# Modulation vectors of a two-block float32 kernel: in column groups, and most of them inside the first input projection

## The reference

```python
m_l = jnp.split((jax.nn.silu(c) @ mod_w[i] + mod_b[i])[:, None, :], 6, -1)      # block 1
hl = _modulate(x, m_l[0], m_l[1])          # layer norm, * (1 + scale) + shift
yl = _hyena(hl, ...)                       # input projection 1024 -> 3072, short and long convolutions, output projection
x  = _ln_affine(ALPHA * x + (1.0 + m_l[2]) * yl, ...)
hl = _modulate(x, m_l[3], m_l[4])
x  = _ln_affine(ALPHA * x + (1.0 + m_l[5]) * _expert_choice_moe(hl, ...), ...)

m_lat = jnp.split(sc @ ada_w[l] + ada_b[l], 6, axis=-1)                         # block 2, condition c
m_ctx = jnp.split(scc @ ada_w[l] + ada_b[l], 6, axis=-1)                        # block 2, condition c_ctx
h_lat = modulate(rms_norm(x, norm1_g[l]), m_lat[0], m_lat[1])                   # then mixer, experts, final norm
```

## Time and profile before

| | |
|---|---|
| median of three runs | 4993.97 us (4990.66 to 4994.40) |
| the profiled execution | 4985.86 us |
| its span, first to last instruction | 4984.2 us |
| TensorE busy (PE) | 4086.8 us, 82% |
| VectorE busy (DVE) | 1827.0 us, 37% |
| ScalarE busy (ACT) | 734.3 us, 15% |
| mean granted TensorE clock | 0.914 of full |
| bytes read from HBM | 692.5 MB |
| setup stage | 0 to 159.6 us |
| first projection | 159.6 to 546.7 us |

### The profile page before, as it was taken

One profiled execution on the slowest core, in us unless ns is written; L12 is line 12 of the kernel. 1 busy time (PEld: TensorE's weight loads), 2 busy tenths in 40 slices (PEclk: granted clock), 3 DMA queues, 4 the chain that ended last, 5 costly groups with the idle time before them and its releaser, 6 DMA issues. The chain is left out here.

```text
span 4984.2 us, 55127 instructions
## 1 busy us (share of the span) xinstructions
PE 4086.8 (82%) x22522; PEld 2294.5 (46%) x22522; DVE 1827.0 (37%) x2640; ACT 734.3 (15%) x1507; POOL 977.9 (20%) x789
## 2 busy tenths in 40 slices
PE   6999765666488899999999997499966899584995
PEld 2444554555343244444444443255444888342442
DVE  3132488888833500000000001444065666234003
ACT  0100111111011000000000000212124333111110
POOL 0000376556620000000000000100021555300110
PEclk9999887888789999999999998799977999796997
DMA  6212100010043788887888885221111000305994
GB/s 228 104 69 94 66 36 36 36 72 36 17 190 117 266 303 320 298 314 289 314 305 301 303 301 209 81 71 60 54 56 64 4 4 4 133 34 196 332 322 164
DMA packets 298090, 773.12 MB, mean 155 GB/s; under 512 B 9400, under 2 KB 40112, under 8 KB 290734
## 3 DMA queue, kind: packets, MB, share of 16 engines
q1 hardware_dynamic: 272434, 656.65, 35.5%
q0 software_dynamic: 24352, 103.06, 6.2%
q10 hardware_dynamic: 1116, 10.71, 0.5%
HBM read 692.50 MB, written 77.88 MB: 155 GB/s over the span
## 5 line engine op out<-in xcount | busy, mean ns | idle before, releaser
L1266 PE MATMUL banks<-moe_ring,moe_xeT 128*128 128x512 f32 x2560 | 1122.2, 594 | 4.4 <-ACT moe_xeT L1320 4.4
L1266 PEld LDWEIGHTS banks<-moe_ring,moe_xeT 128*128 128x128 f32 x2560 | 484.4, 191 | 596.6 <-issue 596.6
L1286 PE MATMUL banks<-moe_ring,moe_hidT 128*128 128x512 f32 x1280 | 565.7, 595 | 21.6 <-ACT moe_hidT L1327 21.6
L1356 DVE TENSOR_TENSOR moe_hid<-moe_silu,banks 128x512 f32<-128x512 f32 x80 | 55.0, 687 | 1294.5 <-PE banks L1266 1294.5
L1286 PEld LDWEIGHTS banks<-moe_ring,moe_hidT 128*128 128x128 f32 x1280 | 240.6, 190 | 320.1 <-issue 290.8
L1235 POOL DMA_INDIRECT d_acc<-moe_ye,chosen x32 | 50.8, 1586 | 1688.9 <-DVE moe_ye L1360 1688.9
L1552 PE MATMUL banks<-hT,w_in_ring 128*128 128x512 f32 (+3 forms) x976 | 362.8, 535 | 4.3 <-ACT hT L1575 4.3
L322 PE MATMUL banks<-hT,w_in_ring 128*128 128x512 f32 x768 | 335.5, 596 | 4.3 <-ACT hT L334 4.3
L521 PE MATMUL banks<-y_folded,dft 128*128 128x256 f32 x512 | 128.1, 417 | 231.0 <-DVE y_folded L687 231.0
L1552 PEld LDWEIGHTS banks<-hT,w_in_ring 128*128 128x128 f32 (+1 forms) x976 | 183.0, 188 | 183.8 <-issue 171.5
L962 PE MATMUL banks<-w_out,mix 128*128 128x512 f32 x512 | 230.3, 608 | 11.1 <-DMA w_out<-d_w_out 10.3
(11 more groups left out here) (437 smaller groups left out, 5209.3 us busy)
## 6 DMA issues: line engine op xcount, KB each, us to landing
moe_ring<-d_wg SPq DMA_DIRECT2D x80, 2048.0 KB, 12.6
moe_ring<-d_wu SPq DMA_DIRECT2D x80, 2048.0 KB, 17.3
moe_ring<-d_wd SPq DMA_DIRECT2D x80, 2048.0 KB, 7.9
mod_w_ring<-d_mod_w SPq DMA_DIRECT2D x24, 1024.0 KB, 5.5
w_out<-d_ada_w POOLq DMA_DIRECT2D x12, 2048.0 KB, 9.3
w_in_ring<-d_hy_w_in SPq DMA_DIRECT2D x6, 2048.0 KB, 8.6
d_seq<-u_staged POOLq DMA_DIRECT2D x12, 1024.0 KB, 4.1
w_in_ring<-d_w_in SPq DMA_DIRECT2D x5, 2048.0 KB, 10.4
```

The costliest lines, as they stand in the source:

```text
L1266: last = nc.tensor.matmul(m.ps[:, 2 * kind + c, :], xeT[:, k, :], up(c, kind)[:, k, :], start=(k == 0), stop=(k == KT - 1))
L1286: last = nc.tensor.matmul(m.ps[:, Y_BANK + h, :], hidT[:, c, i * P:(i + 1) * P], down(c)[:, i, h * BANK:(h + 1) * BANK], start=(fc == 0 an ...
L1356: nc.vector.tensor_tensor(hid[:, j % 2, :], sg[:, j % 2, :], m.ps[:, 2 + j % 2, :], ALU.mult).then_inc(s.hid, 1)
```

## The change

Both matvecs are done in six groups of 2048 columns: groups 0 to 2 are block 1's vector, 3 to 5 block 2's two. The weights are silu(c) (or the two vectors of block 2 in turn) repeated to 32 columns. The four matmuls of one k write to PSUM partitions 0, 32, 64 and 96 of one bank, each with 512 of the 2048 columns as its moving operand. One copy brings the 128 x 512 rows to SBUF and four small matmuls with picked identity columns turn them into columns in bank 7.

Group 0 stays in the setup stage, as 8 MB in four loads without a wait. Groups 1 to 5 are 20 slots of two k (2 MB each), one behind each of the units 1 to 20 of the projection; their ring of two lies in the memory of x, free after the transposes. The loops over kinds of SyncE, ScalarE and TensorE are written out; turns use two banks instead of four; the turn of a kind's last unit stands behind the next kind's first unit; `dft` is loaded early. The additions for parts 2 to 5 and for block 2 stand at the end of the projection stage. The ada chunks leave `mixer_out_stage`.

```diff
+def matvec(nc, m, lhs, k, w):
+    for j in range(4):
+        last = nc.tensor.matmul(m.ps[32 * j:32 * j + 32, ROW_BANK, :], lhs[:, k, :], w[:, j * BANK:(j + 1) * BANK],
+                                start=(k == 0), stop=(k == KT - 1))
+    return last
+
+def rows_to_columns(nc, m, rows, group):
+    pick = m.ident[:].rearrange("p (j x) -> p j x", j=4)
+    for b in range(4):
+        if group < MOD_GROUPS:
+            out, rhs = mod_columns(m, group)[:, b], pick[:, :, 0]
+        else:
+            out, rhs = ada_columns(m, group - MOD_GROUPS)[:, b], pick[:, :, 0:2]
+        last = nc.tensor.matmul(out, rows[:, b * P:(b + 1) * P], rhs, start=True, stop=True)
+    return last
...
@@ setup_stage, SyncE, ScalarE, TensorE
-            for i in rounds(sp, N_MOD_CHUNKS // RING):
-                at = [settled(sp, i * (RING * MOD_CHUNK) + c * MOD_CHUNK) for c in range(RING)]
-                for slot in range(RING):
-                    sp.wait_ge(used[slot], i)
-                    sp.dma_start(ring[:, slot], m.dram["mod_w"][:, :, ds(at[slot], MOD_CHUNK)]).then_inc(ready[slot], 16)
+            for slot in range(MV_SLOTS):
+                sp.dma_start(ring[:, slot], m.dram["mod_w"][:, slot * MV_SLOT_K:(slot + 1) * MV_SLOT_K, 0:MV_COLS]
+                             ).then_inc(ready[slot], 16)
...
+            act.wait_ge(s.row_mm, 1)
+            nc.scalar.copy(row[:], m.ps[:, ROW_BANK, :]).then_inc(s.row, 1)
+            act.wait_ge(s.var, 1)
+            nc.scalar.activation(rstd[:], rstd[:], ACT.Sqrt).then_inc(s.std, 1)
...
+            for k in range(KT):
+                if k % MV_SLOT_K == 0:
+                    pe.wait_ge(ready[k // MV_SLOT_K], 16)
+                last = matvec(nc, m, m.lhs_mod, k, ring[:, k // MV_SLOT_K, k % MV_SLOT_K, :])
+            last.then_inc(s.row_mm, 1)
+            pe.wait_ge(s.row, 1)
+            rows_to_columns(nc, m, row, 0).then_inc(s.col_mm, 1)
...
@@ hyena_in_stage, SyncE
+            load_w(0, 0)
+            load_w(0, 1)
+            sp.wait_ge(s.hT_mm, 2 * KT)
+            load_mv(0)
+            load_mv(1)
             sp.dma_start(m.dft[:], m.dram["dft"]).then_inc(s.tables, 16)
+            for unit in range(UNITS):
+                kind, mt = unit // MT, unit % MT
+                if mt % 4 == 3 and kind + 1 < KINDS:
+                    sp.wait_ge(s.u_mm, 2 * unit + 2)
+                    load_w(kind + 1, mt // 4)
+                n = slot_of(unit)
+                if n is not None and n + 2 < N_SLOTS:
+                    sp.wait_ge(s.mv_mm, n + 1)
+                    load_mv(n + 2)
...
@@ hyena_in_stage, TensorE
+            def matvec_slot(n):
+                group, kp = 1 + n // MV_SLOTS, n % MV_SLOTS
+                pe.wait_ge(mv_in[n % 2], (n // 2 + 1) * 16)
+                if kp == 0 and group > 1:
+                    pe.wait_ge(s.mv_row, group - 1)
+                lhs = m.lhs_mod if group < MOD_GROUPS else m.lhs_ada
+                for j in range(MV_SLOT_K):
+                    last = matvec(nc, m, lhs, kp * MV_SLOT_K + j, mv_ring[:, n % 2, j, :])
+                last.then_inc(s.mv_mm, 1)
...
+            for unit in range(UNITS):
...
+                if unit:
+                    turn(unit - 1)
+                n = slot_of(unit)
+                if n is not None:
+                    matvec_slot(n)
+                before = slot_of(unit - 1)
+                if before is not None and before % MV_SLOTS == MV_SLOTS - 1:
+                    matvec_columns(1 + before // MV_SLOTS)
+            turn(UNITS - 1)
...
@@ hyena_in_stage, ScalarE and VectorE
+                if n is not None and n % MV_SLOTS == MV_SLOTS - 1:
+                    group = 1 + n // MV_SLOTS
+                    act.wait_ge(s.mv_mm, n + 1)
+                    if group > 1:
+                        act.wait_ge(s.mv_col, group - 1)
+                    nc.scalar.copy(mv_rows[:], m.ps[:, ROW_BANK, :]).then_inc(s.mv_row, 1)
...
+                v.wait_ge(s.u_ready, kind * (2 * MT))
...
@@ mixer_out_stage, TensorE
-            if deep:
-                ada(0)
-                ada(1)
             pe.wait_ge(s.out_read, 2 * TT)
...
-            if deep:
-                for c in range(2):
-                    ada_columns(c)
-                    ada(c + 2)
             pe.wait_ge(s.aff, 1)
```

More of the change, by code:

```diff
@@ L30 @@
 N_MOD = 6 * KT
-MOD_CHUNK = 256
-N_MOD_CHUNKS = 6 * D // MOD_CHUNK
 EMB = 33
@@ L296, in _, with turn @@
             pe.wait_ge(s.hT_ready, 2 * KT)
-            def turn(kind, mt):
-                pe.wait_ge(s.conv, kind * MT + mt + 1)
+            def turn(unit):
+                mt = unit % MT
+                pe.wait_ge(s.conv, unit + 1)
                 for par in range(2):
-                    if 2 * mt + par >= 4:
-                        pe.wait_ge(s.staged, kind * (2 * MT) + 2 * mt + par - 3)
+                    n = 2 * unit + par
+                    if n >= 2:
+                        pe.wait_ge(s.staged, n - 1)
@@ L303, in turn @@
                     for j in range(4):
                         last = nc.tensor.transpose(
-                            m.ps[:, 4 + (2 * mt + par) % 4, j * P:(j + 1) * P],
+                            m.ps[:, 4 + par, j * P:(j + 1) * P],
                             uc[:, mt % 2, 4 * P * (j % 2) + 2 * par + j // 2:4 * P * (j % 2 + 1):4], m.ident[:])
                     last.then_inc(s.tr_mm, 1)
[L309 to L321, removed]
-                            last = nc.tensor.matmul(m.ps[:, g % 4, :], ring[:, c, k, (mt % 4) * P:(mt % 4 + 1) * P],
-                                                    hT[:, k, h * BANK:(h + 1) * BANK], start=(k == 0), stop=(k == KT - 1))
-                        last.then_inc(s.u_mm, 1)
-                    if mt:
-                        turn(kind, mt - 1)
-                turn(kind, MT - 1)
@@ new lines, in matvec_columns @@
+            def matvec_columns(group):
+                pe.wait_ge(s.mv_row, group)
+                rows_to_columns(nc, m, mv_rows, group).then_inc(s.mv_col, 1)
+            for unit in range(UNITS):
+                kind, mt = unit // MT, unit % MT
+                c = mt // 4
+                if mt % 4 == 0:
+                    pe.wait_ge(ready[c], (kind + 1) * 16)
+                for h in range(HALF):
+                    g = 2 * unit + h
+                    if g >= 4:
+                        pe.wait_ge(s.u_ready, g - 3)
+                    for k in range(KT):
+                        last = nc.tensor.matmul(m.ps[:, g % 4, :], ring[:, c, k, (mt % 4) * P:(mt % 4 + 1) * P],
+                                                hT[:, k, h * BANK:(h + 1) * BANK], start=(k == 0), stop=(k == KT - 1))
+                    last.then_inc(s.u_mm, 1)
+                if unit:
[6 more added lines that the diff above has]
+                    matvec_columns(1 + before // MV_SLOTS)
@@ L1019, in _ @@
             last.then_inc(s.at_mm, 1)
-            if deep:
-                for c in range(2, ADA_CHUNKS):
-                    ada_columns(c)
-                    if c + 2 < ADA_CHUNKS:
-                        ada(c + 2)
             pe.wait_ge(s.top, 1)
```

175 lines of the change are left out of this document (76 added, 99 removed).

## The result

| | before | after |
|---|---|---|
| median, same chip | 4992.32 us (4988.88 to 4994.40) | 4927.62 us (4927.05 to 4928.70) |
| ratio, 95% interval | | 0.9871 [0.9854, 0.9888] |
| profiled execution / its span | 4985.86 / 4984.2 | 4927.98 / 4926.3 |

The changed kernel is 1.3% faster: 64.7 us by the medians, 57.9 us between the two profiled executions. Forecast was 4938, in a range of 4924 to 4985.

What follows compares the result with a forecast made beforehand. TensorE was taken to bound setup's end and the projection. Gains of 104.9 us less 7.8 of losses and 41.2 for slots gave 55.9 net off the 4994.0 median: 4938.1 us, 8-in-10 range 4924 to 4985.

Steps and rivals of the forecast that it cites:

- setup shorter: Setup stage: last additions follow VectorE's normalising operation at 88.14, not TensorE's matvec at 158.65; 70.5 us less.
- 20 slots: Projection: column groups run together, 1.72 us a slot plus 0.34 for two drains, 2.06 each, 41.2 us lost.
- experts' cold start: After the router stage: without ada matmuls before them the experts start with TensorE cold, 0.7 us lost.
- The row of two tiles: Trace row: 12 records on two 64 x 64 tiles sharing no rows or columns take 2.79 us; basis for the slot price.
- B: Projection rival, half together: next group starts only beside a matmul's second record; slot 4.2 us, total 4981 us; chance 0.10.
- C: Projection rival: groups on shared rows run one behind the other; slot 7.2 us, total 5045, up to 5062; chance 0.16.
- D: Projection rival: hidden slots wait for their loads, 5 us each, about 5038 us; chance 0.04 together with mixtures.
- A step to columns: Projection: four small matmuls turning rows into columns, five times at 0.95 us each, 4.8 us lost.
- The nine additions: Projection's end: nine small VectorE operations stand behind the last stored wait, 1.3 us lost.
- The cold start: Start of the projection: TensorE stands still before the hT phase's 64 transposes, 1.0 us lost.
- the two borders: Projection, between kinds: two TensorE idle times of 3.67 us go, plus 1.1 for the slower clock; 8.4 us gained.
- The cover at the borders: Projection: next kind's bias is ready some 4 us before its turn; a store 4 us later would use that up.

Runs made afterwards that it cites:

- the kernels of one, two and four groups: Changed kernel with each k's four matmuls sent to one 32-column group (5031.77 us), alternating between two (4959.97 us), or unaltered with four (4927.62 us).
- the kernel with three groups in setup: Changed kernel with block 2's slots moved to the router stage and all three block 1 groups computed in setup: 4897.17 us.
- The eight other kernels: Follow-up variants of the changed kernel, altering group count, issue order, or where block 1's and block 2's vectors are computed; 4891.49 to 5031.77 us.
- the other order of issue: Changed kernel with the group as outer loop in a slot, so two matmuls follow each other on one group: 4927.83 us.
- block 2 back in the router stage, in chunks or in groups: Changed kernel with block 2's vectors computed in the router stage, as the old 12 chunks (4928.91 us) or as 12 column-group slots (4902.04 us).
- two or three groups in setup: Changed kernel with block 2's column-group slots in the router stage and two (4891.49 us) or three (4897.17 us) block 1 groups in setup.
- the groups without the move: Changed kernel with block 1's three groups in setup, block 2's 12 old chunks in the router stage, no projection slots: 4923.47 us.

## Why the prediction was right, step by step

| term | forecast | measured |
|---|---|---|
| setup shorter | 70.5 | 159.56 - 88.64 = 70.9 |
| 20 slots | 41.2 (2.06 each) | 39.6 (1.98 each) |
| projection longer | 40.6 | 423.2 - 387.2 = 36.0 |
| router stretch shorter | 26.7 | 121.39 - 94.75 = 26.6 |
| experts' cold start | 0.7 lost | 12.58 to the first matmul, 12.91 before: 0.3 gained |
| stages with unchanged code | 0 | 7.4 lost, then 3.4 gained |
| profiled executions | 55.9 | 57.9 |

*The slot.* The step on which all hung, that records of different column groups start together although they share all rows, is shown by the kernels of one, two and four groups. The row of two tiles gave the right price, but it could not show this step, since its tiles share no rows: choosing it was a bet, put at 0.70, and it was won. The two drains were too much: 0.13 (1.85 - 1.72) is all that shows from a slot to the next unit, and 1.98 the whole price to ScalarE's evacuations. Rivals B and C fell by the same rows: spacings of 12.1 and 15.1 were theirs, 9.93 was measured. D fell because no idle time is shown at a slot.

The Trainium skill, TensorE: Matmul & The Clock Gate, The mechanism, lets a weight load overlap only when its row group differs. The slot rows do not agree: four groups on the same rows take about a quarter of the time of one, 1.92 us against 7.05 for the same 16 records. The same section names a load into a background weight buffer as a second way; no run here shows whether that is what happens. The Trainium skill, same page, Measured speedup vs the span model, has 2.38 times for three column tiles; here four groups gave 3.8 times and two 1.96, so the measurement decides against carrying that loss over.

*The rest of the projection.* Here the forecast was 4.6 us too dear, and the rows divide it. The slots came 1.6 cheaper. A step to columns costs 0.89: the two evacuations around the first one start at 195.99 and 206.81, 10.82 apart, against 9.93 across a slot alone; five are 4.5 against 4.8. The nine additions were put at 1.3 and cost nothing that shows: from the last store's issue to the stage's end are 5.68 us with them, 5.64 before and in the kernel with three groups in setup, which has none there. TensorE's wait in the last turn rose from 3.69 to 4.38, the 0.7 of the forecast. The cold start held too: the first unit starts 12.64 us into the stage (101.28), 11.57 before, 1.1 against 1.0. The first two units then took 27.73 us and not the 29.43 of before, at a granted clock of 1.00 against 0.94. The eight other kernels have 29.25 to 30.73, among them the one with the other order of issue, whose code is the same up to there, with 29.43. So these 1.7 us are luck of this execution. What remains for the two borders is 8.1 us against 8.4.

*The cover at the borders* held, with about 2 us and not 4, and the rows settle why. From the store's issue to the bias that it releases are 6.9 us at both borders of the changed kernel, where a slot load is issued 0.42 us behind the store (249.91). They are 4.7 at the first border of the kernel before, and 4.8 in the five kernels in which no slot load runs beside it (block 2 back in the router stage, in chunks or in groups; two or three groups in setup; the groups without the move). With the slot load issued 2.1 us behind the store (two groups) they are 5.1, and with 5.5 us (one group) 4.8 again. So a slot load issued right behind the store costs it 2 us, which is the delay the forecast named, at half the size that would have used up the cover. The 5.6 us that the forecast took for the store's landing is the way to the stage's end, about 1.2 longer than the wait for the store (4.4 there); the additions fit into that 1.2.

*Setup and router* came out within 0.4 us of their terms. For the router stage the second block's call of the same function was a measurement of "after" in the trace of before. The 0.7 for the experts' cold start was no price of a cold start: from the first load to the first matmul in block 1 the ten profiles have 12.03 to 12.91, with the 12 chunks ahead of it or without.

*What separates 4938 from 4927.6* is mostly no mechanism. I took the sum off the median of three and so added 8.1 us to what the profiled execution would give. The changed kernel's profiled execution lies 0.4 from its own median, and the one before 6.5 below its median. Of the 10.5 us between forecast and result 8.1 are this step, 2.0 the sum itself (57.9 - 55.9), 0.4 the rest. That the sum is so close is in part luck: its terms were some 6 us too pessimistic (4.6 in the projection, 1.0 at the experts, 0.4 in setup), and the stages with unchanged code lost 4.0 that it did not have.

*The unchanged stages.* The 7.4 us lost between projection and router stage are not the change's doing. Nearly the same code in all ten, from the end of the projection to the start of block 1's last normalising operation, took 1021.0 before, 1028.4 after, and 1020.8 to 1025.6 in the profiles of the eight other kernels. A visible part is the start of the output stage, in the timeline of after and then of the kernel with the other order of issue, whose stage is the same:

```profile
1392.56 8.83 PE L1034 MATMUL banks<-w_out,mix 128*128 128x512 f32 x16 [3.18 <-DMA out_bias<-d_b_out]
```

```profile
1389.79 7.13 PE L1038 MATMUL banks<-w_out,mix 128*128 128x512 f32 x16 [0.91 <-DMA out_bias<-d_b_out]
```

TensorE waits 2.3 us longer for one small transfer in one execution, and the next 16 records take 1.7 longer, at a granted clock of 0.81 in the 9 us from 1392.5, against 1.00 in the same stretch of the other. From the experts' first load to the end the ten profiles have 3291.3 to 3295.1. So the two profiled executions can't be compared below some 7 us outside the stages that the change touches; why TensorE waits longer for this small load in some executions stays open.

## What to carry to other kernels

A matvec should be cut into column groups even when all groups share their rows: the gain is nearly the number of groups, 3.8 for four (measured for float32, 32 columns of weights and 512 moving columns only). Cheap work put on the engine that sets a stage's end is still paid in full: moving block 2's vectors swapped 28 us for 25, while the same slots beside VectorE's selection cost nothing, and the best version (two groups in setup, one in the projection, block 2 under the selection) takes 4891.49 us, 36 below the change and 100 below the kernel before. Before a sum is made against a median, look how far the profiled execution lies from it, and keep that distance as a width of the range and not as a term.

## What the runs showed of the hardware

- A slot on a TensorE that otherwise waits can cost nearly twice: 3.64 us and not 1.92 for the same 16 records. In the kernel with block 2 in groups eight of the twelve slots took 3.35 to 3.64 and four 1.92, two of these behind idle times of 1.62 and 1.91. Its windows around two of the slots have a granted clock of 0.50 (its level of 1.2 GHz) for the one that follows 5.23 us of idle time and scattered work, and 1.00 for one behind dense work. It was hidden there.

```profile
core 0: us, PE busy (x) PEld busy (x) DVE busy (x) ACT busy (x) POOL busy (x), PEclk, DMA share, GB/s
...
1538.00:1540.50 2.50, 2.42 (x25) 0.85 (x24) 1.36 (x5) 1.22 (x2) 0.00 (x0) 1.00 0.00 0
1548.00:1552.00 4.00, 3.62 (x16) 0.59 (x16) 3.90 (x6) 0.00 (x0) 0.00 (x0) 0.50 1.01 426
```

- Loads of `mod_w` in rows of 8 KB moved 420 GB/s where they were alone. The chunks of the kernel before, in rows of 1 KB, had 210 GB/s in the earlier trace rows, though there TensorE set their pace.
